# A feed-forward half's first weight high halves, its first Silu and the conditioning row's Silu: another order on ScalarE

## The reference

```
cond = jax.nn.silu(c)
for i in range(4):
    mod = (cond @ ada_w[i] + ada_b[i]).reshape(B, 3, 3, D)
    # sublayer: x + res_w * gate * rms_norm(fn(rms_norm(x) * (1 + scale) + shift))
    x = sublayer(x, 0, lambda hh: swiglu(hh, ffn_w1[i, 0], ffn_w2[i, 0]), 0.5)
    x = sublayer(x, 1, mixer_i, 1.0)
    x = sublayer(x, 2, lambda hh: swiglu(hh, ffn_w1[i, 1], ffn_w2[i, 1]), 0.5)

def swiglu(h, w1, w2):
    gate, up = jnp.split(h @ w1, 2, axis=-1)      # 1024 -> 2 x 2816
    return (jax.nn.silu(gate) * up) @ w2          # 2816 -> 1024
```

## Time and profile before

| | us |
|---|---|
| runs: median (lowest to highest) of 3 | 3639.57 (3628.84 to 3641.31) |
| span of the profiled execution | 3623.5 |
| TensorE busy in it (matmuls) | 3031.8 |
| VectorE, ScalarE, GpSimd busy | 2419.6, 1260.3, 516.0 |

### The profile page before, as it was taken

One profiled execution on the slowest core, in us unless ns is written; L12 is line 12 of the kernel. 1 busy time (PEld: TensorE's weight loads), 2 busy tenths in 40 slices (PEclk: granted clock), 3 DMA queues, 4 the chain that ended last, 5 costly groups with the idle time before them and its releaser, 6 DMA issues. The chain is left out here.

```text
span 3623.5 us, 52173 instructions
## 1 busy us (share of the span) xinstructions
PE 3031.8 (84%) x21162; PEld 2543.3 (70%) x21162; DVE 2419.6 (67%) x4307; ACT 1260.3 (35%) x2037; POOL 516.0 (14%) x305
## 2 busy tenths in 40 slices
PE   7977765665556699888999988999997999997899
PEld 4856752222211399878989886998986898987798
DVE  3677748888898777555768726777735775556554
ACT  1043211111111234364343445344344434344633
POOL 1010025555455200000000050000041000000000
PEclk9987777777777899979999997999997999998999
DMA  8932228999999786414848531867651774553153
GB/s 340 384 138 95 84 88 364 394 398 395 386 409 404 309 353 232 170 46 188 329 187 351 206 141 47 350 226 308 266 193 61 281 276 171 184 188 113 51 196 126
DMA packets 123103, 854.18 MB, mean 236 GB/s; under 512 B 17301, under 2 KB 18581, under 8 KB 21013
## 3 DMA queue, kind: packets, MB, share of 16 engines
q1 hardware_dynamic: 85748, 582.69, 42.0%
q0 software_dynamic: 36864, 268.45, 18.2%
q10 hardware_dynamic: 288, 0.26, 0.0%
HBM read 850.24 MB, written 1.11 MB: 235 GB/s over the span
## 5 line engine op out<-in xcount | busy, mean ns | idle before, releaser
L193 DVE TENSOR_TENSOR w_lo<-w_ring,w_hi 128x2048 fp32r<-128x2048 f32 x300 | 686.4, 2290 | 508.1 <-ACT w_hi L188 506.2
L268 PE MATMUL ps<-h_hi,w_hi 128*128 128x256 f32 x3328 | 954.9, 287 | 49.8 <-DVE h_lo L459 26.2
L269 PE MATMUL ps<-h_lo,w_hi 128*128 128x256 f32 x3328 | 950.9, 286 | 0.0
L270 PE MATMUL ps<-h_hi,w_lo 128*128 128x256 f32 x3328 | 950.4, 286 | 0.0
L188 ACT ACTIVATE w_hi<-w_ring 128x2048 fp32r<-128x2048 f32 x330 | 629.7, 1913 | 654.7 <-PE ps L270 634.9
L268 PEld LDWEIGHTS ps<-h_hi,w_hi 128*128 128x128 f32 x3328 | 643.8, 193 | 59.6 <-DVE h_lo L459 29.0
L269 PEld LDWEIGHTS ps<-h_lo,w_hi 128*128 128x128 f32 x3328 | 644.0, 194 | 3.2
L270 PEld LDWEIGHTS ps<-h_hi,w_lo 128*128 128x128 f32 x3328 | 643.7, 193 | 0.0
L2955 PE MATMUL ps<-expert_rows,expert_diag 128*128 128x512 f32 x412 | 289.3, 843 | 228.0 <-ACT expert_diag L2996 228.0
L193 POOL TENSOR_TENSOR w_lo<-w_ring,w_hi 128x2048 fp32r<-128x2048 f32 x30 | 138.2, 4622 | 2251.7 <-ACT w_hi L188 2251.7
L2955 PEld LDWEIGHTS ps<-expert_rows,expert_diag 128*128 128x128 f32 x412 | 92.6, 247 | 416.9 <-ACT expert_diag L2996 339.8
(11 more groups left out here) (461 smaller groups left out, 4215.7 us busy)
## 6 DMA issues: line engine op xcount, KB each, us to landing
w_ring<-in_w_stream SPq DMA_DIRECT2D x376, 1024.0 KB, 4.8
a_ring<-in_a_stream SPq DMA_DIRECT2D x108, 1024.0 KB, 7.2
a_ring<-in_t_stream SPq DMA_DIRECT2D x36, 1024.0 KB, 10.0
a_ring<-in_m_stream SPq DMA_DIRECT2D x8, 1024.0 KB, 7.1
alibi<-in_alibi SPq DMA_DIRECT2D x3, 2048.0 KB, 9.0
cond_row<-in_cond_row SPq DMA_DIRECT2D x8, 512.0 KB, 3.8
expert_rows<-in_experts,expert_idx POOLq DMA_INDIRECT x206, 11.8
gates<-mod_rows SPq DMA_DIRECT2D x3, 1024.0 KB, 5.8
```

The lines of the kernel that those rows point to most:

```text
L193: pool.tensor_tensor(self.w_halves(n)[1], self.w_item(n), self.w_halves(n)[0], ALU.subtract).then_inc(self.lo_made, 1)
L268: pe.matmul(out, stationary[0], moving[0], start=start, stop=False)
L269: pe.matmul(out, stationary[0], moving[1], start=False, stop=False)
L270: return pe.matmul(out, stationary[1], moving[0], start=False, stop=stop)
```

## The change

Only ScalarE's loop at the beginning of each half changes: the high half of item n is now made before the condition on item 3 is looked at, and the conditioning row's Silu has a condition of its own, at item 4. The order becomes: high half of item 3, `silu(0)`, high half of item 4, the row's Silu, `silu(1)`, high half of item 5.

```
             for n in range(core.split_issued, start):
-                if n == gate_item(0) + S_SLOTS:
-                    silu(0)
-                    if n_mod:
-                        act.wait_ge(cond_in.sem, cond_in.at(16))
-                        act.activation(cond_row[:], cond_row[:], ACT.Silu).then_inc(cond_made.sem, 1)
                 if n == gate_item(1) + S_SLOTS:
                     silu(1)
                 core.split_hi(act, n)
+                if n == gate_item(0) + S_SLOTS:
+                    silu(0)
+                if n == gate_item(0) + S_SLOTS + 1 and n_mod:
+                    act.wait_ge(cond_in.sem, cond_in.at(16))
+                    act.activation(cond_row[:], cond_row[:], ACT.Silu).then_inc(cond_made.sem, 1)
```

## The result

| | median, us | lowest to highest | runs |
|---|---|---|---|
| kernel before | 3635.14 | 3628.84 to 3641.31 | 4 |
| changed kernel | 3594.28 | 3586.68 to 3616.58 | 4 |

The ratio is 0.9894, 95% interval 0.9864 to 0.9923. The sign was right, the size and the range were wrong. The profiled executions differ by 26.9: spans of 3623.5 and 3596.6.

What follows compares the result with a forecast made beforehand. TensorE was taken as the bound, stalled at weight 3 in the first six halves. The control's 23.2 us, less 0.6, plus 1.6, gave 24.2 off the median 3639.57: 3615.4 us, range 3603 to 3627.

Steps and rivals of the forecast that it cites:

- The chain DMA, row Silu, high half, low half, TensorE: Beginning of the first six halves: TensorE stalls at weight 3 through ScalarE's wait for the conditioning row, 3.04 to 2.54 us.
- the cover of some 2 us at weight 5: VectorE finishes weight 5's low half at +15.2 and TensorE wants it at +17.3, leaving 2.1 us.
- step (1): Weight 3's high half ahead of the table load: low half done at +4.24, wanted by TensorE at +5.87, 1.6 us left.
- the pause at weight 3: Even the seventh half waits 0.33 us there where 0.12 would do: 0.2 in each of eight halves, 1.6 gained.
- The other two terms: 23.2 us for six halves against the seventh as control; less 0.6, the first six being 0.1 longer each from weight 6.
- The clock's share of 5.6: Of the 23.2 us in the first six halves, 5.6 is slow clock behind three stalls and 17.6 delay.
- I take that distance as unchanged: Whole program: the profiled span lies 16.1 us under the median of the runs shown, and would still do so.
- the gain isn't taken back: Weight loads in the halves land as before; the slowest, weight 8, lands at +22.9, its products start at +34.6.
- B: Stalls in the halves go but slow clock stretches only move: 18.6 us off, 3621; chance 0.18.
- C: No gain, 3639: full DMA engines make TensorE wait for a later weight; sign, ScalarE waiting for w_ring DMA; chance 0.08.
- D: Slower, 3665: late modulation data delays the dots and weight 5's low half, 4.3 us in six halves; chance 0.03.
- E: Larger gain, 3605: a typical execution has more slow clock stretches than the profiled one; chance 0.08.

Runs made afterwards that it cites:

- experiment 12: Changed kernel with SP issuing weights 6 and 7 ahead of the first two modulation pieces instead of behind them: 3640.01 us in one run.
- experiment 3: Kernel before with only weight 3's high half moved first, the row's Silu still ahead of weight 4's high half: median 3594.43 us, ratio 0.9922.
- experiment 4: Kernel before with only the row's Silu moved behind the high halves of weights 3 and 4, first Silu still first: 3610.82 us, ratio 0.9958.
- row_behind: Same run as experiment 4: kernel before with only the row's Silu moved behind the high halves of weights 3 and 4: 3610.82 us, ratio 0.9958.
- before_again: Kernel before, unedited, traced again and timed against itself: median 3628.77 us in its own 12 runs, ratio 1.0012.
- after: The changed kernel in its first comparison with the kernel before: median 3594.28 us in 4 runs, ratio 0.9894.
- experiment 1: Same run as before_again: kernel before, unedited, timed against itself: median 3628.77 us in its own 12 runs, ratio 1.0012.

## Why the prediction was right or wrong, point by point

**Right: where the time is lost and what the order does.** The chain DMA, row Silu, high half, low half, TensorE was read rightly; every time given for the new order came true to about 0.1 us, but for TensorE's start of weight 5 (+17.0 for +17.3); the cover of some 2 us at weight 5 (1.9 measured for 2.1) is real (experiment 12). Of the change's two parts the first gives the whole 25.9 alone (experiment 3), as step (1) says, and the second alone 22.6 (experiment 4).

**Right within 9%: the halves.** Forecast 24.2, measured 25.9 in the first pair and 26.4 against the mean of three traces of before. H1 to H6 are 169.07 where 169.25 was implied. The term that was too small is the pause at weight 3 in the earlier trace rows, put at 0.2 in each of eight halves, 1.6 in all: it was worth 0.38 in seven and 0.66 in the eighth (169.35 less 168.69), 3.3 in all, which makes the 24.2 into 25.9. The other two terms held: 0.1 is what row_behind's H1 to H6 have over H7. The clock's share of 5.6 fits the other traces: the second and the third of before sum to 0.7 more.

**Wrong: "I take that distance as unchanged", the baseline.** This is the step that failed. The forecast was made in microseconds from the median of three runs, 3639.57. Over all comparisons the kernel before has a median of 3626.1 (65 runs, 3607 to 3641, standard deviation 8.8; before_again's own 12 leave the median where it is). On the three chips of the later comparisons it is 3629.1, 3624.5 and 3624.1; which chip had the first runs isn't on record, so whether they were a high draw or a slower chip is open. The profiled execution's own time was the span plus 1.8, by the profiled run of after (3598.36 for 3596.6), so the 16.1 between span and median were hardly a fixed cost: 14 of them were the difference between the one execution that was profiled and three from the upper part of the spread. The 13.5 from 3639.57 to 3626.1 are the largest part of the 21.1 us by which the time was missed. A range of 24 us around a number that is a median of three from a spread of 33 was too narrow by this alone.

**Wrong: "the gain isn't taken back", nor added to, outside the halves.** The sum ended at the halves. In code that the change doesn't touch, x5 was 3 us shorter in five of seven traces, x3 was at 202 in the same five (and in one of the kernel before's three, the first), and row_behind's pieces were 15 to 20 longer. The sum put all of this at nothing. Over all runs the change is worth 29.5 us (means 3626.1 and 3596.6, 65 and 23 runs; standard error 2.5), 0.81%, of which the halves explain 26.4; the 3 left are no more than that error. With the scatter of x1 reduced it is 32.9 (means of 12 and 11 runs; standard error 1.9), and there the rest, 6.5, is larger than the error. This term accounts for some 4.4 us of the miss, by medians (28.6 less 24.2).

**Chance.** The first four runs of after had 3594.28, later ones 3595.48 and 3598.15; the median of all 23 is 3597.5. That is 3.2 us. 13.5, 4.4 and 3.2 are the 21.1. That the measured gain of 40.9 is so far over the 28.6 of all runs is this and the high baseline together; the later runs show no such gain.

**The rivals.** B, slow stretches that only move: in the halves they went, and nothing of the 5.6 came back there; outside they did move, in the traces of the unshifted changed kernel mostly in its favour. C: I had named a row of ScalarE waiting for `w_ring` as its sign. The row is there in the changed kernel (and with 9.0 us in 2 waits in the kernel before):

```profile
ACT w_hi L188 <- DMA w_ring<-in_w_stream: 62.2, 14, 5.6
```

It was a wrong sign. Weight 6's high half needs a slot that weight 3's products free, and these end some 5 us earlier now (+11.5 for +17), so ScalarE waits for the load instead and starts at +13.1. Weight 6's low half is done at +19.2, TensorE wants it at about +22.8 and doesn't wait. D holds as a mechanism only. E said 3605 for a reason that fell (experiment 1); its number was nearer for others.

**The Trainium skill's rule** on the clock ("TensorE: Matmul & The Clock Gate", Part 1) said that slow matmuls differ in number between executions. That I let it touch only the 5.6 us at the stalls was the same mistake in small: where the clock falls differs from trace to trace all over the program, x1 above all, and so it bears on the baseline. The traces agree with the rule: 25.3 or 14.9 us for the same 128 matmuls.

**What stays open:** which chip or chance made the first baseline high, what makes the stretch before half 1 differ by up to 13 us, why x3, x5 and x7 are 202.0, 189.0 and 233.9 together in five traces and all longer in two, and why row_behind fell so steadily on the dear side. That the clock differs with the length is seen in x5, x7 and x1; by what rule a start time would pick the outcome isn't shown.

## What to carry to other kernels

At the beginning of a stage, make first what the busiest engine wants next, and put a step that waits for a DMA issued in this very stage behind it: here one instruction moved to the front was worth 26 us over the eight halves, 22.6 of them for no longer standing behind the wait. Price a stall on TensorE from a twin stage that lacks it rather than from the wait's own length, since in 11 of 18 cases here the clock's fall behind it came on top. And before forecasting in microseconds, look at the runs' spread: take the forecast as a ratio, and widen the range by what a median of three can be off.

The fastest version here is the changed kernel with 16 fillers: 3585.8 median of 11 runs (3582.9 to 3595.2), against 3597.5 of 23 for the changed kernel and 3626.1 of 65 for the kernel before.

## What the runs showed of the hardware that I had not expected

- Through 128 matmuls of 60 columns, one behind the other, the granted clock fell from 1.00 to 0.50 in 12 of 20 cases, 2.0 to 2.9 us behind the first, though TensorE had no idle time among them: 25.3 us (the mean clock 0.56) instead of 14.9. In the ten traces without fillers x1 was dear (244 to 249) in nine and x7 (245 to 247) in three. With sixteen wide matmuls among them, at 3.1 us, it stayed at 1.00 in 6 of 6, with four at the beginning in 2 of 2.
- An idle time of TensorE of 2.5 to 3.4 us was followed by a stretch at the lower level in 11 of 18 cases, one of 4.2 to 4.5 us in 6 of 6.
- A delay of 1.1 us in one stage came with 3.1 us more in the next, unchanged one (one run), and an order whose halves are 3.3 us longer came out 15 us slower in the median.
